# Sums over k of 16 adaLN column groups: from TensorE to VectorE, in a two-block transformer kernel

## What is computed

```python
shift, scale, gate = jnp.split(jax.nn.silu(c) @ ada_w[l] + ada_b[l], 3, axis=-1)
shift_c, scale_c, gate_c = jnp.split(jax.nn.silu(c_ctx) @ ada_w[l] + ada_b[l], 3, axis=-1)
h = rmsnorm(x, norm_g[l]) * (1.0 + scale[:, None]) + shift[:, None]
hc = rmsnorm(xc, norm_g[l]) * (1.0 + scale_c) + shift_c
# ... projections, attention, pooling, Fourier mixing, out ...
x_new = x + gate[:, None] * out
if not last:
    xc = xc + gate_c * outc
```

## Time and profile before

| | us |
|---|---|
| median of 3 runs | 2350.48 |
| lowest, highest | 2348.18, 2351.04 |
| span of the profiled execution | 2348.8 |

### The profile page before, as it was taken

The page is one execution under the profiler, slowest core; times in us unless marked ns, Lnnn a source line. Parts: engine busy times, 40 slices in busy tenths (PEclk is TensorE's granted clock), DMA queues, the critical chain, the costliest instruction groups (busy, mean ns, idle before and its releaser), DMA issues.

```text
span 2348.8 us, 30025 instructions
## 1 busy us (share of the span) xinstructions
PE 2272.0 (97%) x11859; PEld 1830.4 (78%) x11859; DVE 1288.4 (55%) x2030; ACT 1042.1 (44%) x1596; POOL 269.0 (11%) x326
## 2 busy tenths in 40 slices
PE   5899999999999999999999998999999999999998
PEld 2477777777777867678888887888888888888887
DVE  3354523332332264555776776667765777567764
ACT  2233333332322255445554565555544555345553
POOL 1010100000010122100020324111100111001111
PEclk9999999999999999999999998999999999999999
DMA  9974433445655475634566544565655555555553
GB/s 350 341 263 157 149 126 114 139 132 167 243 179 172 134 276 194 237 96 159 181 207 204 172 143 153 179 196 180 189 195 190 187 185 184 198 188 188 188 189 116
DMA packets 322427, 437.14 MB, mean 186 GB/s; under 512 B 13848, under 2 KB 220112, under 8 KB 321264
## 3 DMA queue, kind: packets, MB, share of 16 engines
q1 hardware_dynamic: 316800, 413.19, 53.2%
q0 software_dynamic: 3392, 16.90, 1.9%
q10 hardware_dynamic: 2096, 5.15, 0.6%
HBM read 428.89 MB, written 6.29 MB: 185 GB/s over the span
## 4 chain that ended last, share of the span: by engine, by line
PE 87%; DVE 4%; ACT 3%; DMA 3%; issue 1%; POOL 1%; SPq 0%; ACTq 0%; POOLq 0%
PE ps L1334 24%; PE ps L1335 12%; PE ps L1309 9%; PE ps L1311 8%; PE ps L1310 8%; PE ps L1329 5%; PE ps L1330 5%; PE ps L1331 5%; PE ps L1289 3%; PE ps L1383 1%; DVE SPL L1784 1%; ACT SPL L1540 1%; PE ps L1400 1%; DMA RAW<-in_ada_w_dram 1%; PE ps L1390 1%
## 5 line engine op out<-in xcount | busy, mean ns | idle before, releaser
L1784 DVE TENSOR_TENSOR SPL<-RAW,SPL 128x1024 fp32r<-128x1024 f32 x592 | 751.6, 1274 | 598.4 <-ACT SPL L1540 596.1
L1334 PE MATMUL ps<-HS,SPL 128*128 128x512 f32 x2688 | 957.7, 401 | 10.8 <-DVE SPL L1784 7.8
L1540 ACT ACTIVATE SPL<-RAW 128x1024 fp32r<-128x1024 f32 x592 | 622.1, 1055 | 493.2 <-PE ps L1311 170.9
L1335 PE MATMUL ps<-HS,SPL 128*128 128x256 f32 x2688 | 755.3, 281 | 0.0
L1334 PEld LDWEIGHTS ps<-HS,SPL 128*128 128x128 f32 x2688 | 507.7, 189 | 135.4 <-DVE SPL L1784 5.6
L1335 PEld LDWEIGHTS ps<-HS,SPL 128*128 128x128 f32 x2688 | 510.5, 190 | 2.0 <-issue 1.7
L1309 PE MATMUL ps<-SPL,HS 128*128 128x512 f32 x960 | 396.8, 413 | 12.2 <-DVE SPL L1784 5.3
L1311 PE MATMUL ps<-SPL,HS 128*128 128x512 f32 x960 | 377.1, 393 | 0.0
L1310 PE MATMUL ps<-SPL,HS 128*128 128x512 f32 x960 | 376.9, 393 | 0.0
L1309 PEld LDWEIGHTS ps<-SPL,HS 128*128 128x128 f32 x960 | 182.1, 190 | 75.5 <-issue 17.5
L1310 PEld LDWEIGHTS ps<-SPL,HS 128*128 128x128 f32 x960 | 182.3, 190 | 41.8 <-issue 6.3
(11 more groups left out here) (281 smaller groups left out, 1689.3 us busy)
## 6 DMA issues: line engine op xcount, KB each, us to landing
RAW<-in_w_in_dram SPq DMA_DIRECT2D x208, 512.0 KB, 5.7
RAW<-in_ada_w_dram SPq DMA_DIRECT2D x192, 512.0 KB, 4.9
RAW<-in_ffn_w_up_dram SPq DMA_DIRECT2D x192, 512.0 KB, 3.5
RAW<-in_w_out_dram SPq DMA_DIRECT2D x96, 512.0 KB, 4.5
RAW<-in_ffn_w_down_dram SPq DMA_DIRECT2D x96, 512.0 KB, 4.1
x_spill<-XT POOLq DMA_DIRECT2D x2, 2048.0 KB, 15.3
XT<-x_spill POOLq DMA_DIRECT2D x1, 4096.0 KB, 17.4
MM<-in_x_dram ACTq DMA_DIRECT2D x2, 1024.0 KB, 10.8
```

What stands on the lines that cost most here:

```text
L1334: mm(PS[b][:, :], wr, hh, start=k == 0, stop=False, skip_group_check=True)
L1335: m = mm(PS[b][:, 256:512], wl, hh[:, 0:256], start=False, stop=k == KT - 1, skip_group_check=True)
L1540: act(SPL[:, (n - 1) % NSPL, 0, :], raw_of(i), ACT.Copy).then_inc(s_hi, 1)
L1784: tt(w[:, 1, :], raw_of(s["i"]), w[:, 0, :].bitcast(F32), ALU.subtract).then_inc(s_lo, 1)
```

## The change

- The 128 adaLN chunks behind the opening become chunks of form "sum" (`ada_sums` takes the place of `ada_group` there). VectorE multiplies each k tile (128 x 512, in `RAW`) by the per-partition scalar from `CW` and adds it to an accumulator, for each vector: 4 instructions per chunk for two vectors, 2 for the gate groups of layer 1, which now keep one vector only.
- The accumulators lie in slots 6 and 7 of `RAW` (`NSUM` = 6), in turns from group to group. From the first sum to 7 chunks behind the last, loads use slots 0 to 5 alone; `place_raw` gives every chunk the slot used longest ago. A slot with a sum chunk comes free when VectorE has added it.
- When a group is summed, TensorE turns each vector's accumulator (four transposes into bank 6, `sum_turn`), and VectorE reduces the bank to four columns, then adds the bias as before. ScalarE has no part in it.
- `mixed` puts one sum behind every weight chunk, and in layer 0's projections two behind every twelfth: 69 sums there, 28 in w_out, 31 in layer 1. `FILL` is 0. Layer 1's groups come in the order 4 to 7, 0 to 3, 8 to 11.
- Some semaphores are merged (`s_tab`, `s_dft`, `s_ap`), and `s_chunk` counts multiplied chunks alone.

```diff
-FILL = 4
+FILL = 0
+NSUM = 6
...
+        def place_raw():
+            sums = [i for i, c in enumerate(queue) if c.shape == 1]
+            users = [[] for _ in range(NRAW)]
+            for i in range(len(queue)):
+                free = range(NSUM if sums[0] <= i < sums[-1] + NRAW else NRAW)
+                slot = min(free, key=lambda j: users[j][-1] if users[j] else j - NRAW)
+                raw_slot.append(slot)
+                raw_nth.append(len(users[slot]) + 1)
+                raw_before.append(users[slot][-1] if users[slot] else None)
+                users[slot].append(i)
...
         def load_ahead():
             while at["loaded"] < len(queue):
-                i = at["loaded"] - NRAW
-                last = []
-                if i >= 0 and queue[i].shape:
-                    if i >= at["taken"]:
+                i, last = at["loaded"], []
+                b = raw_before[i]
+                if b is not None:
+                    if b >= at["taken" if queue[b].shape > 1 else "pos"]:
                         return
...
+                    last = [(s_lo, split_no[b])] if queue[b].shape > 1 else after_chunk[b]
...
+                if c.shape == 1:
+                    sum_chunk(i, c)
+                    continue
...
+            done = []
+            for v in range(g.vectors):
+                done.append((s_acc[v], at["summed"][v]))
+                at["summed"][v] += 2
+            put("ada_sum", i=i, kc=c.kc, half=g.half, before=done, last=last if c.kc == 0 else [])
+            after_chunk[i] = [(s_acc[g.vectors - 1], at["summed"][g.vectors - 1])]
...
-        def mixed(main, left):
+        def mixed(main, left, more=0):
             seq = []
-            for c in main:
+            for i, c in enumerate(main):
                 seq.append(c)
-                if len(seq) % 4 == 2:
-                    seq.extend(left[:2])
-                    del left[:2]
+                n = 2 if more and i % more == more - 1 else 1
+                seq.extend(left[:n])
+                del left[:n]
             return seq
...
+        def ada_sums(l, g):
+            vectors = 1 if l and g >= 8 else 2
...
+                while len(hi) < 3:
+                    hi.append(idle)
+                for v in range(vectors):
+                    hi.insert(3 + v, turn(v))
...
-        left = [c for g in range(8, 12) for c in ada_group(0, g)] + [c for g in range(12) for c in ada_group(1, g)]
+        left = [c for g in range(8, 12) for c in ada_sums(0, g)] + [c for g in (*range(4, 8), *range(4), *range(8, 12)) for c in ada_sums(1, g)]
...
-        lay_out(main0[0] + mixed(main0[1], left))
+        lay_out(main0[0] + mixed(main0[1], left, 12))
...
-        lay_out(mixed(outs1, left))
+        lay_out(outs1)
...
+                elif kind == "sum_turn":
+                    e.wait_ge(*s["sums"])
+                    for b in range(4):
+                        o = slice(b * 128, (b + 1) * 128)
+                        m = turn(PS[6][:, o], sums_of(s["half"], s["v"])[:, o], IDN[:, :])
+                    m.then_inc(s_accT, 1)
...
+                elif kind == "ada_sum":
+                    i, kc, half = s["i"], s["kc"], s["half"]
+                    for sm, v in new((s_c, 1), *s["last"]):
+                        e.wait_ge(sm, v)
+                    e.wait_ge(s_raw[raw_slot[i]], 16 * raw_nth[i])
+                    for kk in range(2):
+                        w = raw_of(i)[:, kk * 512:(kk + 1) * 512]
+                        for v, (sm, before) in enumerate(s["before"]):
+                            acc, c = sums_of(half, v), CW[:, 4 * kc + 2 * kk + v:4 * kc + 2 * kk + v + 1]
+                            if kc == 0 and kk == 0:
+                                ts(acc, w, c, None, ALU.mult).then_inc(sm, 1)
+                            else:
+                                e.wait_ge(sm, before + kk)
+                                stt(acc, w, c, acc, ALU.mult, ALU.add).then_inc(sm, 1)
+
+                elif kind == "sum_turn":
+                    l, g, v = s["l"], s["g"], s["v"]
+                    a = ADA[:, l, 4 * g:4 * g + 4, :]
+                    e.wait_ge(s_accT, n)
+                    nc.vector.tensor_reduce(a[:, :, v], PS[6][:, :].rearrange("p (b q) -> p b q", b=4), AX_X, ALU.add).then_inc(s_adaS, 1)
+                    if s["end"]:
+                        ada_columns(s, a[:, :, 0:s["vectors"]], s["vectors"])
```

More of the change, by code:

```diff
@@ L231, in two_block_program @@
         slots = [(i, []) for i in range(4)]
-        at = {"loaded": 0, "taken": 0, "split": 0, "used": 0, "pos": 0, "ahead": AHEAD}
+        at = {"loaded": 0, "taken": 0, "split": 0, "used": 0, "pos": 0, "ahead": AHEAD, "multiplied": 0, "summed": [0, 0], "sums": 0}
+        raw_slot, raw_nth, raw_before = [], [], []
+        after_chunk = {}
+        sums_last, sums_turns = {}, {}
         split_no, chunk_split = {}, {}
@@ L286, in run_ahead @@
                     split_no[i], chunk_split[at["split"]] = at["split"], i
-                    last = [(s_chunk, chunk_split[at["split"] - NSPL] + 1)] if at["split"] > NSPL else []
+                    last = after_chunk[chunk_split[at["split"] - NSPL]] if at["split"] > NSPL else []
                     put("split", i=i, last=last)
@@ L338, in run_chunks, with chunk_multiplied, sums_first, sum_chunk @@
                     put("mm", i=i, c=c, inputs=inputs, after=after, banks=range(part * half, (part + 1) * half), end=part == parts - 1, src=c.group.src)
-                at["pos"] = i + 1
-                at["used"] += c.shape > 0
+                chunk_multiplied(i)
                 if c.then:
                     c.then()
+        def chunk_multiplied(i):
+            at["pos"] = i + 1
+            at["multiplied"] += 1
+            after_chunk[i] = [multiplied()]
+            at["used"] += chunks[i].shape > 0
+        def sums_first(half):
+            b = max(j for j in range(at["pos"]) if raw_slot[j] == NSUM + half)
+            return [(s_lo, split_no[b])] if queue[b].shape > 1 else after_chunk[b]
+        def sum_chunk(i, c):
+            g = c.group
+            if c.kc == 0:
+                if g.half not in sums_last:
+                    sums_last[g.half] = sums_first(g.half)
+                last = sums_last[g.half]
+                while last and last[0] is None:
+                    hi.pop(0)()
+                    last = sums_last[g.half]
+            done = []
[4 more added lines that the diff above has]
+            after_chunk[i] = [(s_acc[g.vectors - 1], at["summed"][g.vectors - 1])]
+            at["pos"] = i + 1
+            if c.then:
+                c.then()
         def staged(tasks):
@@ L368, in two_block_program, with after, turn, f @@
         ada_ready, s2_ready = {}, {}
+        def ada_sums(l, g):
+            vectors = 1 if l and g >= 8 else 2
+            half = ada_sums.count % 2
+            ada_sums.count += 1
+            def after():
+                sums = [(s_acc[v], at["summed"][v]) for v in range(vectors)]
+                at["sums"] += vectors
+                sums_last[half] = [None]
+                def turn(v):
+                    z = {}
+                    def f():
+                        s = put("sum_turn", l=l, g=g, v=v, half=half, sums=sums[v], after=use(6), end=v == vectors - 1, vectors=vectors)
+                        sums_turns[l, g, v] = s["n"]
+                        bank_last[6] = [(s_adaS, tick("ada_sum_out"))]
+                        if v == vectors - 1:
+                            sums_last[half] = [(s_accT, s["n"])]
+                            s["out"] = tick("ada_out_columns")
+                            ada_ready[l, g] = (s_ada, s["out"])
+                            if 4 <= g < 8:
+                                s2_ready[l, g - 4] = (s_s2, tick("s2"))
+                        s["sum_no"] = count["ada_sum_out"]
+                    return f
+                while len(hi) < 3:
+                    hi.append(idle)
+                for v in range(vectors):
+                    hi.insert(3 + v, turn(v))
+            cs = group("sum", "ada", I["ada_w"][l, :, :], g * 512, [], after, side=0)
+            cs[0].group.half, cs[0].group.vectors = half, vectors
+            return cs
+        ada_sums.count = 0
         def ada_group(l, g, side=0):
@@ L380, in spread @@
             def spread(slot):
-                s = put("ada_turn", slot=slot, l=l, g=g, after=use(7))
+                s = put("ada_turn", slot=slot, l=l, g=g, after=use(7), out=tick("ada_out_columns"), sum_no=tick("ada_sum_out"))
                 give(slot, (s_adaT, s["n"]))
-                ada_ready[l, g] = (s_ada, s["n"])
+                ada_ready[l, g] = (s_ada, s["out"])
                 bank_last[7] = [ada_ready[l, g]]
@@ L1422, in tensor @@
                     lv, gi = lay[s["l"]], s["gi"]
-                    for sm, v in new(*s["ready"], (s_dft[s["l"]], 16)):
+                    for sm, v in new(*s["ready"], (s_dft, 16 * (s["l"] + 1))):
                         e.wait_ge(sm, v)
```

(2 more changed lines are left out.)

76 lines of the change are left out of this document (42 added, 34 removed).

## The result

Slower: 2460.47 us (2457.62 to 2462.80, 4 runs) against 2350.54 us (2348.18 to 2351.04, 4 runs); the ratio is 1.047, 95% interval 1.0456 to 1.0485. The forecast was 2331 us, so it missed by 129 us, and the result lies outside its range.

What follows compares the result with a forecast made beforehand. TensorE, busy 97% of 2348.8 us, was taken as the bound; -76.8 + 5.3 + 10 + 6 + 24 + 12 = -19.5 gave span 2329.3, plus 1.7: 2331 us. Forecast case 2311 to 2345 (chance 0.45), full range 2286 to 2366.

Steps and rivals of the forecast that it cites:

- What is removed and added on TensorE: On TensorE, 128 adaLN chunks at 0.6 us go, 76.8 us; 12 more turns at 0.44 us add 5.3 us.
- VectorE's price: On VectorE, sums add 305 us (2.65 per two-vector chunk, 1.58 per one-vector chunk) and 28 reductions 20 us.
- the same chain: Layer 0's ring: load, both split halves, side work and sum take 9.75 us plus side against 10.9, hidden on average.
- its landing: In the ring's chain, two loads in a row land after 4.9 us, between 3.5 and 6.2.
- The lateness: TensorE held up: layer 0 +10 us at head norms and +6 at paired sums; layer 1 24 and 12 us.
- Layer 1's q stretch: Layer 1's first 16 chunks: the load chain takes 5.0 us per chunk where TensorE needs 3.5, costing 24 us.
- pooling: Layer 1's 8 pooling chunks: the chain takes 5.3 us where TensorE needs 3.65, costing 12 us.
- The k/v chunks need 5.8 and hide it: Layer 1's 8 k/v chunks: 5.8 us needed per chunk, so the load chain is hidden and adds nothing.
- A half chunk of matmuls, 2.7 us, lies between the two and covers the 0.7 us of the reduction: A group's two turns share one PSUM bank; the second's wait is covered unless VectorE is behind, then counted as lateness.
- Rival 2: VectorE sets layer 0's pace: 69 sums each delay TensorE 0.9 us, 62 us instead of 16, giving 2377; chance 0.23.
- Rival 1: All VectorE work is hidden: 2294 us with layer 1's 15 us, 2279 with none; chance 0.22.
- a full gain: Whole kernel, if VectorE hid everything: 71.5 us gained, 2279 us.

Runs made afterwards that it cites:

- b2: Kernel after, with weight and sum chunks given 4 and 2 ring slots of their own and each kind's loads issued independently; 2386.97 us, ratio 1.0163 to before.
- c3: b2 without the second vector's sums, and only 32 of 512 columns summed behind a group's first chunk; 2331.70 us, ratio 0.992 to before.
- a4: Kernel after, with the second vector's turn in PSUM bank 7 instead of bank 6; 2446.15 us, ratio 1.0391 to before.
- c1: b2 with the second vector's turn in PSUM bank 7 instead of bank 6; 2368.90 us, ratio 1.0078 to before.
- a3: Kernel after without the second vector's sums, and only 32 of 512 columns summed behind a group's first chunk; 2392.64 us, ratio 1.0163 to before.
- b1: Kernel after, with weight and sum chunks given 3 ring slots each and each kind's loads issued independently; 2388.87 us, ratio 1.0171 to before.

## Why the prediction was wrong, point by point

- **What is removed and added on TensorE: right.** The opening alone has adaLN matmuls left. The first turn of the stall above stands 0.24 us behind the matmul before it, the next matmul 0.35 later and the one after 0.31: 0.43 us, where 0.44 was forecast.
- **VectorE's price: right.** 312 us against 325; the multiply-adds have a median of 0.747 and a mean of 0.772 us, between the ends of 0.66 and 0.79. Four in a row come at 0.68 each. What was missed is that a few are slower beside GpSimd (below).
- **The step that failed: "In layer 0 the same chain is 4.9 + 1.06 + 1.14 + 2.65 + side = 9.75 + side, against 10.9 plus TensorE's own side work: hidden on average."** The chain was written out, and its landing was right (4.9 forecast; in layer 0 the medians are 4.8 for w_in and 5.1 for w_out). But 1.15 us of slack in 10.9 is none once side steps stand in it: in the stall above they are 1.65 us of evictions and 1.6 us by which the sum is longer than its 2.65. The lateness was priced at 36 us in layer 1 and 16 us in layer 0, where the end came another 109 us later than that. The runs put 73 us on the order of the loads (b2), 49 of them in layer 0, as its end moved from 892.2 to 842.9, and another 55 on VectorE's sums (c3), 39 of them in layer 0, whose end moved to 804.3.
- **Layer 1's q stretch (24 us) and pooling (12 us): right in size. "The k/v chunks need 5.8 and hide it": wrong.** The row of q, then of k/v, in the kernel after (columns of the earlier trace rows):

```profile
896.20:976.30 80.10, 56.34 (x216) 44.50 (x217) 58.49 (x92) 34.83 (x57) 19.29 (x21) 0.81 0.55 185
976.30:1034.50 58.20, 48.47 (x209) 39.12 (x208) 36.47 (x58) 24.00 (x41) 13.90 (x14) 0.94 0.52 173
```

q runs at 5.0 us per chunk, as forecast, and pooling at 5.5 against 5.3. There is some luck in q's match: the clock of 0.81 makes its matmuls longer, which the chain didn't have, and TensorE's largest wait there is for the heads that VectorE norms and rotates (L2011, 12.5 us), not for the split (4.7 us). The k/v chunks took 58.2 us where the forecast had 46. Between the two landmarks the kernel after took 323.1 us against 286.9 before, 36 more, where the forecast had about 16.5 more; 12 of the 20 us of miss are the k/v chunks.
- **"A half chunk of matmuls, 2.7 us, lies between the two and covers the 0.7 us of the reduction": wrong.** It covers the reduction, not VectorE's queue ahead of it. It was priced at 0 and "part of the lateness priced below"; the waits are 33.8 us, the cost 14 to 18 us (a4, c1).
- **The clock: no term at all.** 58 us of the loss are matmuls at the lower clock. Every term of lateness should have been made larger by what follows a wait: in the stall shown, 4.5 us of waiting brought another 2.6 us lost in slower matmuls.
- **The rivals.** Rival 2, VectorE's pace (2377), had the right sign and some of the mechanism: VectorE's time costs 55 to 68 us (a3, c3). Its price was worked out without loads, so it too lay 83 us short. Rival 1 is excluded by the result, and c3 shows how far off it was: even with the sums thinned out and the loads in free order, the kernel takes 2331.7 us, not 2279 to 2294. That c3 lands on the forecast's 2331 is an accident; it does not do the work.
- **Open.** The 52 us between c3 and a full gain: 9.2 us of bank waits, 17 of longer matmuls, and waits that weren't separated, perhaps from the 84 us of work that VectorE keeps there. A ring of eight slots beside the accumulators wasn't tried.

## What to carry to other kernels

A chain through a shared ring with an in-order issuer is to be priced by its slack against the side work that can fall into one turn of it, not by averages: VectorE, busy some 70% here, was late for somebody in every stretch. Before giving a tuned kernel's ring slots away, ask what each load would stand behind, and let loads of different consumers have slots and an order of their own. In this kernel a wait of TensorE of 4.5 us cost 7.1, so a few long waits cost more than a share of busy time suggests.

## What the runs showed of the hardware

**GpSimd slows VectorE's sums.** The same four multiply-adds take 2.73 us when GpSimd is still, and 4.82 us when two of its additions run beside them. From the timeline of the kernel after:

```profile
760.42 2.73 DVE L1940 SCALAR_TENSOR_TENSOR RAW<-RAW,CW 128x512 f32<-128x512 f32 x4
...
781.57 4.82 DVE L1940 SCALAR_TENSOR_TENSOR RAW<-RAW,CW 128x512 f32<-128x512 f32 x4
...
781.61 3.56 POOL L2406 TENSOR_TENSOR TMP<-TMP 128x512 f32<-128x512 f32 x2 [23.40 <-ACT TMP L1774]
```

The Trainium skill, GPSIMD Engine Reference, Specifications, says that GpSimd shares its SBUF interfaces with VectorE, with contention for instructions with two SBUF inputs; a multiply-add of weights and accumulator has two. The trace agrees, and the forecast didn't weigh it. It matters in places more than in sum: six sums of the run stand beside those additions (L2406) and take 3.2 to 4.8 us instead of 2.7, some 10 us of VectorE's time in all. One of them is the sum in the stall above. Beside GpSimd's small additions (L2374) 26 multiply-adds kept their 0.75 us.

**The clock after a wait.** While TensorE stood still for 4.5 us the stretch shows 0.81, then 0.50 and 0.57 for some 5 us of dense matmuls, then 1.00. Across the runs the mean clock roughly follows the idle time: 0.990 at 77 us, 0.985 at 111, 0.978 at 132, 0.962 at 202; 0.979 at 150 (b1) doesn't fall in line.
